# Moving the seven seven-product units of each FFN down-projection pass

## The chip, the cores and the metric

The kernel runs on one core of one Trainium2 chip. The metric is the device time of one execution in microseconds (us), the median of several runs. TensorE is called PE below, VectorE DVE, ScalarE ACT, GpSimd POOL, SyncE SP.

## The reference, cut to what matters

The program is a two-layer decoder trunk on a sequence of 256 positions with a model width of 2048, all in float32: a recurrent block (RG-LRU) and an FFN, then an attention block on shared compressed keys and values and a second FFN. Each FFN is

```
def swiglu(hn, w_in, w_out):
    u = hn @ w_in
    return (jax.nn.silu(u[..., :D_FF]) * u[..., D_FF:]) @ w_out
```

with D_FF = 5632. The change touches only how the last product of this line, `(...) @ w_out` (256x5632 by 5632x2048, the down projection), is cut up, in both FFNs.

## The kernel before, in words

**Precision.** Every float32 operand is split into a high part (`w_hi`, `act_hi`, rounded to fp32r by an ACT copy) and a low part (`raw_lo`, `w_lo`, `act_lo`: the operand minus its high part, by DVE). One block product is three matmuls of 128x128 by 128x512: high by high, high by low, low by high (`product`, L1731).

**Units.** The FFN weights come in loads of 1024 KB, one per unit, through four buffers in turn (`raw[n % 4]`). A unit of the down projection is 256 rows of the weights by 1024 columns, that is 2x2 blocks of weights (two row blocks, two column blocks) by 2x2 blocks of activations (two row blocks of the same index, two token tiles). A plain unit does the 2x2 block product in the usual way: 8 block products, 24 matmuls (`plain_unit`). A sum unit does it with 7 block products, 21 matmuls, of sums of blocks (`sum_unit`; a Strassen-like scheme); its products go into two sets of four PSUM banks, `result` and `shared`.

**What a unit costs the other engines.** For a plain unit ACT makes `w_hi` (L555) and DVE makes `raw_lo` (L1005). For a sum unit of the down projection DVE first makes sums of activation blocks (four small instructions, L1083 to L1089) and of weight blocks (four, L1041 to L1046) in `down_sums` and `sums`; ACT makes the high parts of all of them (L616 to L625); DVE makes the low parts in `down_split` and `split_sums` (L1101, L1051, L1055, L1058). The last of these, L1058, or L1005 for a plain unit, increments `w_lo_done`, for which PE waits before the unit. In every second iteration DVE also makes the low part of four activation tiles (`stationary`, L1031), which PE needs before the next even unit (`st_lo`).

**The passes.** The down projection of an FFN is 44 units, two passes of 22 (`PASS_UNITS`), each pass for 1024 of the 2048 output columns. `DOWN_SUMS` names the units of a pass that are sum units; all others are plain. Units are counted from 0 to 43 below: unit 22 is the first of the second pass.

**Order.** There is no planner. Each engine runs its instructions in the order written; semaphores connect them. In `two_pass`, iteration n of DVE and of ACT prepares unit n + 4: DVE does `stationary` if n is odd, then `down_sums(n + 4)` if that is a sum unit, then `down_split(n + 4)`. ACT does the same with its parts. SP issues the load of unit n when PE has finished unit n - 4 (`chunk_used`); `down_sums` also waits for that, and for the load (`raw_in`). At the end of a pass DVE adds the `shared` banks to `h` (`shared_to_h`, in the iteration of the last sum unit, which stays 17) and the `result` banks (`results_to_h`, L1121, in iteration 21). In the first FFN's second pass ACT also makes squares of `h` (`squares`, L584) in iteration 23.

**The hand-over.** The down projection's first four units are prepared by the last block of the up projection (`up`, `body(FB - 1, False)`, DVE from L1205 on). There DVE does, in order: `shared_add`, the split of unit 1, `down_sums` of unit 2, `result_out` (L1210, L1212, and the gating L1190, after ACT's silu L687), the split of unit 2, the split of unit 3. PE transposes the gated block (`transpose_g`, L1724) in the middle of unit 1.

**Buffers.** Sum tiles of weights alternate between two places (`g_no % 2`), sums of activations between three (`g_no % 3`), where `g_no` counts the sum units.

Of the kernel before, what the change touches and what calls it, by code (L numbers as in the profile page):

```python
# [33 lines left out]
FB = FF // W  # L34
# [47 lines left out]
S_UNITS = (2, 4, 6)  # L82
# [1 line left out]

PASS_UNITS = 2 * FB
DOWN_UNITS = 2 * PASS_UNITS
DOWN_SUMS = (2, 5, 7, 10, 12, 15, 17)

UP_TILES, DOWN_TILES = (0, 1, 2, 3), (0, 2, 1, 3)
SUM_BLOCKS = S_BLOCKS + 2  # L90
SUMS = len(S_UNITS) * S_BLOCKS + 2 * len(DOWN_SUMS)

# [17 lines left out]
def build_program(nc, a, out):  # L110
    x, positions = a["x"], a["positions"]
    ctx = ExitStack()
    with ctx:
# [322 lines left out]
        def stat(c, n=1):  # L436
            return stats[:, c:c + n]
# [66 lines left out]
        def is_sum(i, u):  # L504

            return u in S_UNITS and not (isinstance(i, int) and i in (0, FB))
# [5 lines left out]
        def down_sum(n):  # L512

            return n % PASS_UNITS in DOWN_SUMS

        def down_sum_no(n):

            half, v = divmod(n, PASS_UNITS)
            return len(DOWN_SUMS) * half + DOWN_SUMS.index(v)

        def down_unit_no(f, n):

            return SUMS * f + 3 * S_BLOCKS + down_sum_no(n)
# [20 lines left out]
        def _(act):  # L544
# [55 lines left out]
            def gT_out(i, n, banks):  # L600

                act.wait_ge(gT_mm, n)
                for a, bank in enumerate(banks):
                    e = A.activation(feat[:, bass.ds(4 * i + 2 * a, 2), :],
                                     bank[:, :].rearrange("p (a b) -> p a b", a=2), ACT.Copy)
                e.then_inc(gT_act, 1)

            def split_sums(m, s, q, e, tiles=UP_TILES, g_no=None):
# [4 lines left out]
                if g_no is not None:  # L613
                    act.wait_ge(g_sum, g_no + 1)
                    j = g_no % (2 * len(DOWN_SUMS)) % 3
                    A.activation(s_hi[:, j, :, :], s_raw[:, j, :, :], ACT.Copy).then_inc(g_sum_hi, 1)  # L616
# [10 lines left out]
            def down_split(f, n):  # L627
# [3 lines left out]
                elif down_sum(n):  # L631
                    g_no = down_sum_no(n)
                    split_sums((DOWN_C[2 * f + 1] + n) // 4, n % 4, down_unit_no(f, n), g_no % 2,
                               DOWN_TILES, 2 * len(DOWN_SUMS) * f + g_no)
                else:
                    split((DOWN_C[2 * f + 1] + n) // 4, n % 4)

            def two_pass(f):
# [9 lines left out]
                for n in range(DOWN_UNITS - 4):  # L648
                    half, v = divmod(n, PASS_UNITS)
                    if n == 0:  # L650
                        gT_out(FB - 1, FB * (f + 1), ps[0:2])
                    if v == DOWN_SUMS[-1]:
                        p1_out(n, half)
# [342 lines left out]
        def _(dve):  # L996
# [77 lines left out]
            def down_sums(f, n):  # L1074

                d, g_no = 2 * f + 1, down_sum_no(n)
                v, o, j = n % PASS_UNITS, 2 * len(DOWN_SUMS) * f + g_no, g_no % 3
                m, s = (DOWN_C[d] + n) // 4, n % 4
                dve.wait_ge(gT_act, FB * f + v // 2 + 1)
                dve.wait_ge(chunk_used, 4 * m + s - 3)  # L1080
                a11, a21 = feat[:, 2 * v, 0:P], feat[:, 2 * v, P:SEQ]
                a12, a22 = feat[:, 2 * v + 1, 0:P], feat[:, 2 * v + 1, P:SEQ]
                V.tensor_tensor(s_raw[:, j, 0, :], a22, a21, ALU.subtract).then_inc(g_sum_step, 1)  # L1083
                V.tensor_tensor(s_raw[:, j, 2, :], a11, a21, ALU.subtract)
                dve.wait_ge(g_sum_step, 2 * o + 1)
                V.scalar_tensor_tensor(out=s_raw[:, j, 1, :], in0=s_raw[:, j, 0, :], scalar=-1.0, in1=a11,
                                       op0=ALU.mult, op1=ALU.subtract).then_inc(g_sum_step, 1)
                dve.wait_ge(g_sum_step, 2 * o + 2)
                V.tensor_tensor(s_raw[:, j, 3, :], a12, s_raw[:, j, 1, :], ALU.add).then_inc(g_sum, 1)  # L1089
                sums(m, s, down_unit_no(f, n), g_no % 2, DOWN_TILES)  # L1090
# [97 lines left out]
            def up(f, c0, d):  # L1188
                def gated(t, src):
                    return V.scalar_tensor_tensor(out=gtmp[:, t, :], in0=src, scalar=stat(RS + 2 * (d + 1) + t),  # L1190
                                                  in1=gtmp[:, t, :], op0=ALU.mult, op1=ALU.mult)

                def following(i, u):

                    i, u = i + u // 4, (u + 4) % 8
                    m, s = 2 * i + ((c0 + u) // 4), u % 4
                    if isinstance(i, int) and i == FB:
                        down_split(f, u)
                    elif is_sum(i, u):
                        if u != S_UNITS[0]:  # L1200
                            sums(m, s, unit_no(f, i, u), s // 2)
                        split_sums(m, s, unit_no(f, i, u), s // 2)
                    else:
                        split(m, s, to=raw_lo)

                def result_out(i, result):

                    dve.wait_ge(chunk_used, 8 * i + (c0 + 8))
                    for t in range(NT):
                        V.tensor_tensor(gtmp[:, t, :], gtmp[:, t, :], result[2 * t][:, :], ALU.add).then_inc(c_gate, 1)  # L1210
                    for t in range(NT):
                        k = V.tensor_tensor(mix[:, t, :], result[2 * t + 1][:, :], mix[:, t, :], ALU.subtract)  # L1212
                    k.then_inc(r_done, 1)
                    dve.wait_ge(r_done, i + S_BLOCKS * f)
                    dve.wait_ge(silu_done, i + (FB * f + 1))
                    for t in range(NT):
                        k = gated(t, mix[:, t, :])
                    k.then_inc(g_done, 1)

                def body(i, odd):  # L1220
                    result, shared = banks_of(odd)
                    for u in range(8):
                        if u in (3, 4) and isinstance(i, int) and i == FB - 1:
                            stationary(u - 3, act_slot(u - 3), DOWN_G0[d + 1] + u - 2)
                        if u == 6:
                            shared_add(shared, i + (SUM_BLOCKS * f - 1), i + (FB + 2) * f)
                            following(i, 5)
                            if isinstance(i, int) and i == FB - 1:
                                down_sums(f, S_UNITS[0])
                            else:  # L1230
                                sums(2 * i + (c0 // 4 + 2), 2, unit_no(f, i + 1, 2), 1)
                            continue
                        if u == 7:
                            result_out(i, result)
                            following(i, 6)
                        if u != 5:
                            following(i, u)

                for u in range(8):
                    if u == 1:  # L1240
                        act_tiles(d, 3)
                    if u == 2:

                        dve.wait_ge(side_copied, 3 * f + 3)
                        a11, a21 = side_a[:, :, 0, 0:P], side_a[:, :, 0, P:SEQ]
                        a12, a22 = side_a[:, :, 1, 0:P], side_a[:, :, 1, P:SEQ]
                        V.tensor_tensor(side[:, :, 0, :], a22, a21, ALU.subtract).then_inc(u_side, 1)
                        V.tensor_tensor(side[:, :, 2, :], a11, a21, ALU.subtract).then_inc(u_done, 1)
                        dve.wait_ge(u_side, 2 * f + 1)
                        V.scalar_tensor_tensor(out=side[:, :, 1, :], in0=side[:, :, 0, :], scalar=-1.0, in1=a11,  # L1250
                                               op0=ALU.mult, op1=ALU.subtract).then_inc(u_side, 1)
                        dve.wait_ge(u_side, 2 * f + 2)
                        V.tensor_tensor(side[:, :, 3, :], a12, side[:, :, 1, :], ALU.add).then_inc(side_done, 1)
                    if u == 4:
                        dve.wait_ge(side_hi, f + 1)
                        V.tensor_tensor(s_lo, side, s_hi.bitcast(F32), ALU.subtract).then_inc(side_lo, 1)
                    if u == 6:
                        sums(c0 // 4 + 2, 2, unit_no(f, 1, 2), 1)
                        continue
                    if u == 7:  # L1260

                        dve.wait_ge(chunk_used, c0 + 8)
                        dve.wait_ge(silu_done, FB * f + 1)
                        gated(0, ps[1][:, :])
                        gated(1, ps[3][:, :]).then_inc(g_done, 1)
                        following(0, 6)
                    following(0, u)
                with dve.Fori(0, S_BLOCKS // 2 - 1) as j:
                    body(2 * j + 1, True)
                    body(2 * j + 2, False)  # L1270
                body(FB - 2, True)
                body(FB - 1, False)

# [846 lines left out]
```

## Time and profile before

| | |
|---|---|
| time, median of 3 runs (lowest, highest) | 1996.44 us (1996.17, 1996.79) |
| profiled execution: its own time | 1996.43 us |
| profiled execution: its span | 1994.6 us |
| PE busy, share of the span | 1974.2 us, 99% |
| PE weight load busy | 1683.8 us, 84% |
| DVE busy | 1649.1 us, 83% |
| ACT busy | 1136.6 us, 57% |
| first FFN, down projection (units 0 to 43) | about 786 to 1020 us |
| second FFN, down projection | about 1759 to 1991 us |
| TensorE's granted clock | 1.00 of full speed in every slice |

Busy is the time in which an engine has at least one instruction under way. Matmuls are pipelined, with modelled ends: of two matmuls in a row the second starts 0.23 us after the first though each is shown with 0.39 us, so PE looks busy across pauses shorter than that, and pauses of PE are read from the starts of its matmuls. DVE and ACT instructions that wait for nothing also start a little before the one in front has ended.

### The profile page before, as it was taken

Reading aid. Unit: us, or ns where it says so; the run is one execution under the profiler, and the core shown is the slowest. Engines: PE = TensorE matmul, PEld = TensorE weight load, DVE = VectorE, ACT = ScalarE, POOL = GpSimd, SP = SyncE. Lnnn points to the kernel's source line nnn. Section 1 sums busy time; section 2 is a strip of 40 time slices with the busy share of each in tenths; the row PEclk is TensorE's granted clock in tenths of the full one; section 3 lists DMA queues with packets and bytes.
Section 4 is the critical chain, followed back from the end, with each engine's and each line's share of the span. In section 5 each row is a group of like instructions: output and inputs, shape, how many; then the busy total and the mean of one; then the engine's idle time right before and its main releaser. Section 6 shows DMA issues by size and latency. Waiting matters only on the chain.

```text
span 1994.6 us, 26207 instructions
## 1 busy us (share of the span) xinstructions
PE 1974.2 (99%) x9907; PEld 1683.8 (84%) x9907; DVE 1649.1 (83%) x1849; ACT 1136.6 (57%) x1356; POOL 76.5 (4%) x113
## 2 busy tenths in 40 slices
PE   7999999999999999999999999999999999999999
PEld 7999988888888888888898888888888888888887
DVE  6868655788888889999976886468988898899897
ACT  5478445555555556556676664455555555556564
POOL 1140200000000000000001110000000000000000
PEclk9999999999999999999999999999999999999999
DMA  8564663556556565565565435355656556655554
GB/s 278 170 206 158 206 212 115 199 193 202 197 191 209 191 204 194 195 206 192 209 201 169 127 126 185 111 189 192 205 194 205 194 191 208 193 196 203 200 202 168
DMA packets 159488, 378.21 MB, mean 190 GB/s; under 512 B 6154, under 2 KB 10516, under 8 KB 159028
## 3 DMA queue, kind: packets, MB, share of 16 engines
q1 hardware_dynamic: 158960, 376.02, 56.4%
q0 software_dynamic: 272, 1.13, 0.2%
q8 instruction: 48, 0.79, 0.2%
q14 instruction: 28, 0.23, 0.0%
q10 hardware_dynamic: 180, 0.05, 0.0%
HBM read 375.08 MB, written 2.10 MB: 189 GB/s over the span
## 4 chain that ended last, share of the span: by engine, by line
PE 89%; issue 5%; DVE 2%; ACT 1%; DMA 1%; POOL 1%; POOLq 0%; SPq 0%; DVEq 0%; ACTq 0%
PE bank L1731 75%; PE bank L1912 10%; PE bank L1692 2%; PE bank L1724 1%; PE bank L1715 1%; DVE w_lo L1005 0%; POOL stats L1676 0%; DMA h<-in_x 0%; ACT w_hi L555 0%; DMA raw<-in_ffn_w_in 0%; DMA raw<-in_ffn_w_out 0%; PE bank L1894 0%; ACT gtmp L687 0%; ACT w_hi L618 0%; ACT w_lo L621 0%
## 5 line engine op out<-in xcount | busy, mean ns | idle before, releaser
L1731 PE MATMUL bank<-w_hi,act_hi 128*128 128x512 f32 x1840 | 720.2, 391 | 1.7 <-issue 1.5
L1731 PE MATMUL bank<-w_hi,act_lo 128*128 128x512 f32 x1840 | 716.4, 389 | 0.0
L555 ACT ACTIVATE w_hi<-raw 128x2048 fp32r<-128x2048 f32 (+2 forms) x271 | 509.8, 1884 | 331.6 <-DMA raw<-in_ffn_w_in 149.5
L1731 PE MATMUL bank<-raw_lo,act_hi 128*128 128x512 f32 x1584 | 616.4, 389 | 0.0
L1005 DVE TENSOR_TENSOR raw_lo<-raw,w_hi 128x2048 fp32r<-128x2048 f32 x176 | 401.8, 2288 | 112.6 <-ACT w_hi L555 110.5
L1731 PEld LDWEIGHTS bank<-w_hi,act_hi 128*128 128x128 f32 x1840 | 345.5, 188 | 74.9 <-issue 2.6
L1731 PEld LDWEIGHTS bank<-w_hi,act_lo 128*128 128x128 f32 x1840 | 345.4, 188 | 72.1
L1731 PEld LDWEIGHTS bank<-raw_lo,act_hi 128*128 128x128 f32 x1584 | 297.5, 188 | 60.5
L1005 DVE TENSOR_TENSOR w_lo<-raw,w_hi 128x2048 fp32r<-128x2048 f32 (+2 forms) x95 | 211.8, 2240 | 84.3 <-ACT w_hi L555 84.0
L1055 DVE TENSOR_TENSOR raw_lo<-raw,w_hi 128x2048 fp32r<-128x2048 f32 x88 | 201.0, 2284 | 0.0
L618 ACT ACTIVATE w_hi<-raw 128x1024 fp32r<-128x1024 f32 x88 | 93.0, 1057 | 130.0 <-DMA raw<-in_ffn_w_in 107.9
L1731 PE MATMUL bank<-w_lo,act_hi 128*128 128x512 f32 x432 | 153.9, 389 | 0.0
L1731 PE MATMUL bank<-w_lo 128*128 128x512 f32 x528 | 148.2, 389 | 0.0
L1912 PE MATMUL bank<-act_hi,w_hi 128*128 128x256 f32 x512 | 145.6, 284 | 0.0
L1912 PE MATMUL bank<-act_lo,w_hi 128*128 128x256 f32 x512 | 145.1, 283 | 0.0
L1912 PE MATMUL bank<-act_hi,w_lo 128*128 128x256 f32 x512 | 145.1, 283 | 0.0
L1731 PE MATMUL bank<-w_hi,w_lo 128*128 128x512 f32 x352 | 122.7, 389 | 0.0
L1731 PEld LDWEIGHTS bank<-w_lo 128*128 128x128 f32 x528 | 99.1, 188 | 20.6
L621 ACT ACTIVATE w_lo<-t_raw 128x1024 fp32r<-128x1024 f32 x88 | 92.5, 1051 | 35.7 <-DVE t_raw L1042 35.7
L1051 DVE TENSOR_TENSOR w_lo<-t_raw,w_lo 128x1024 fp32r<-128x1024 f32 x88 | 107.4, 1220 | 0.0
L1912 PEld LDWEIGHTS bank<-act_hi,w_hi 128*128 128x128 f32 x512 | 98.6, 193 | 0.1
L1912 PEld LDWEIGHTS bank<-act_lo,w_hi 128*128 128x128 f32 x512 | 98.6, 192 | 0.0
(230 smaller groups left out, 2440.5 us busy)
## 6 DMA issues: line engine op xcount, KB each, us to landing
raw<-in_ffn_w_in SPq DMA_DIRECT2D x176, 1024.0 KB, 5.3
raw<-in_ffn_w_out SPq DMA_DIRECT2D x88, 1024.0 KB, 4.9
raw<-in_lru_w_in SPq DMA_DIRECT2D x32, 1024.0 KB, 5.4
raw<-in_lru_w_out SPq DMA_DIRECT2D x16, 1024.0 KB, 5.4
raw<-in_w_o SPq DMA_DIRECT2D x16, 1024.0 KB, 5.0
raw<-in_w_ukv SPq DMA_DIRECT2D x8, 1024.0 KB, 5.4
raw<-in_w_uq SPq DMA_DIRECT2D x8, 768.0 KB, 4.5
raw<-in_w_dkv SPq DMA_DIRECT2D x8, 576.0 KB, 4.3
```

The lines of the kernel that those rows point to most:

```text
L555: A.activation(flat_chunk(w_hi, s, size), flat_chunk(raw, s, size), ACT.Copy).then_inc(w_hi_done, 1)
L618: A.activation(w_hi[s][:, first, :], raw[s][:, first, :], ACT.Copy)
L621: A.activation(sum_hi_tiles(e)[:, 0:2, :], sum_tiles(t_raw, e)[:, 0:2, :], ACT.Copy).then_inc(sum_hi, 1)
L1005: V.tensor_tensor(flat_chunk(to, s, size), flat_chunk(raw, s, size), flat_chunk(w_hi, s, size).bitcast(F32), ALU.subtract).then_inc(w_lo_d ...
L1051: V.tensor_tensor(sum_tiles(w_lo_t, e)[:, 0:2, :], sum_tiles(t_raw, e)[:, 0:2, :], sum_hi_tiles(e)[:, 0:2, :].bitcast(F32), ALU.subtract)
L1055: V.tensor_tensor(flat_chunk(raw_lo, s, KC * W), flat_chunk(raw, s, KC * W), flat_chunk(w_hi, s, KC * W).bitcast(F32), ALU.subtract)
L1692: i = T.matmul(outs[t], x_part, wp, start=first and n == 0, stop=last and n == 2)
L1715: i = T.transpose(hT_psum(d, b, q)[:, t * P:(t + 1) * P], h[:, t, k * P:(k + 1) * P], ident[:, :])
L1724: i = T.transpose(banks[q // 2][:, (q % 2) * SEQ + t * P:(q % 2) * SEQ + (t + 1) * P], gtmp[:, t, q * P:(q + 1) * P], ident[:, :])
L1731: i = T.matmul(bank[:, :], x_part, w_part, start=first and n == 0, stop=last and n == 2)
L1912: i = T.matmul(lru_bank(idx, q), w_part, x_part, start=first and kk == kks[0] and n == 0, stop=last and kk == kks[-1] and n == 2)
```

## The change

`DOWN_SUMS` gets other numbers: there are seven sum units in each pass, as before, but at other places. The first sum unit of a down projection is now unit 4, which `two_pass` prepares in its iteration 0; so the last block of the up projection no longer makes the sums of unit 2.

```
-DOWN_SUMS = (2, 5, 7, 10, 12, 15, 17)
+DOWN_SUMS = (4, 6, 8, 11, 13, 15, 17)
...
                         if u == 6:
                             shared_add(shared, i + (SUM_BLOCKS * f - 1), i + (FB + 2) * f)
                             following(i, 5)
-                            if isinstance(i, int) and i == FB - 1:
-                                down_sums(f, S_UNITS[0])
-                            else:
+                            if not (isinstance(i, int) and i == FB - 1):
                                 sums(2 * i + (c0 // 4 + 2), 2, unit_no(f, i + 1, 2), 1)
                             continue
```

In units from 0 to 43: before, the sum units are 2, 5, 7, 10, 12, 15, 17, 24, 27, 29, 32, 34, 37, 39; after, 4, 6, 8, 11, 13, 15, 17, 26, 28, 30, 33, 35, 37, 39. The same holds for both FFNs. The loads and their order are the same.

## Rows read from the trace of the kernel before

**Rows 1.** Page: busy time, share of span and instructions of each engine

```profile
PE 1974.2 (99%) x9907; PEld 1683.8 (84%) x9907; DVE 1649.1 (83%) x1849; ACT 1136.6 (57%) x1356; POOL 76.5 (4%) x113
```

**Rows 2.** Windows: stretch, length; busy time of PE, PEld, DVE, ACT, POOL; clock; DMA

```profile
820.00:850.00 30.00, 30.00 (x134) 24.86 (x133) 29.80 (x34) 19.39 (x21) 0.00 (x0) 1.00 0.62 211
```

**Rows 3.** Chain that ended last, in order of time: start, length, what

```profile
498.38 41.53 PE bank L1731 x183
...
798.25 0.74 issue
...
891.40 1.15 DVE act_lo L1031
892.59 112.67 PE bank L1731 x495
...
1770.95 0.74 issue
```

**Rows 4.** PE's timeline around units 1 and 2: start, length, engine, line, operation

```profile
793.96 0.39 PE L1731 MATMUL bank<-w_hi,act_lo 128*128 128x512 f32 x1
794.40 0.33 PE L1724 MATMUL bank<-ident,gtmp 128*128 128x128 f32 x1
...
797.86 0.39 PE L1731 MATMUL bank<-w_hi,act_lo 128*128 128x512 f32 x1
798.99 0.47 PE L1731 MATMUL bank<-w_hi,act_hi 128*128 128x512 f32 x1 [0.74 <-issue]
```

**Rows 5.** DVE's timeline in the hand-over from the up to the down projection

```profile
786.39 0.29 DVE L1083 TENSOR_TENSOR t_raw<-feat_all 128x128 f32<-128x128 f32 x1
...
789.98 1.27 DVE L1210 TENSOR_TENSOR gtmp<-gtmp,bank 128x512 f32<-128x512 f32 x2
...
792.93 1.42 DVE L1190 SCALAR_TENSOR_TENSOR gtmp<-utmp,stats,gtmp 128x512 f32<-128x512 f32 x2 [0.48 <-ACT gtmp L687]
...
798.20 0.68 DVE L1058 TENSOR_TENSOR w_lo<-t_raw,w_lo 128x512 fp32r<-128x512 f32 x1
```

**Rows 6.** DVE's timeline: one sum unit (5), one plain unit (6), one stationary

```profile
804.34 0.28 DVE L1083 TENSOR_TENSOR t_raw<-feat_all 128x128 f32<-128x128 f32 x1
...
805.27 0.69 DVE L1041 TENSOR_TENSOR t_raw<-raw 128x512 f32<-128x512 f32 x1
...
807.93 0.68 DVE L1101 TENSOR_TENSOR w_lo<-t_raw,w_lo 128x512 fp32r<-128x512 f32 x1
...
811.88 0.69 DVE L1058 TENSOR_TENSOR w_lo<-t_raw,w_lo 128x512 fp32r<-128x512 f32 x1
812.48 2.29 DVE L1005 TENSOR_TENSOR raw_lo<-raw,w_hi 128x2048 fp32r<-128x2048 f32 x1
814.69 1.22 DVE L1031 TENSOR_TENSOR act_lo<-feat_all,act_hi 128x1024 fp32r<-128x1024 f32 x1
815.82 0.28 DVE L1083 TENSOR_TENSOR t_raw<-feat_all 128x128 f32<-128x128 f32 x1
```

**Rows 7.** Timeline at unit 17: DVE's last instruction for it, PE's first matmul

```profile
874.80 0.69 DVE L1058 TENSOR_TENSOR w_lo<-t_raw,w_lo 128x512 fp32r<-128x512 f32 x1
...
876.63 0.39 PE L1731 MATMUL bank<-w_hi,act_hi 128*128 128x512 f32 x1
```

**Rows 8.** Timeline of SP and ACT: loads of units 4 and 20, first reader

```profile
791.66 0.37 SPq L362 DMA_DIRECT2D raw<-in_ffn_w_out  x1
...
876.82 0.37 SPq L362 DMA_DIRECT2D raw<-in_ffn_w_out  x1
...
881.99 1.92 ACT L555 ACTIVATE w_hi<-raw 128x2048 fp32r<-128x2048 f32 x1 [3.85 <-DMA raw<-in_ffn_w_out]
```

**Rows 9.** Timeline at the second pass's start: DVE's result additions, ACT's squares

```profile
911.94 2.47 DVE L1121 TENSOR_TENSOR h<-h,bank 128x512 f32<-128x512 f32 x4
...
917.20 0.61 ACT L584 ACTIVATE utmp<-h 128x512 f32<-128x512 f32 x1
...
919.76 0.19 ACT L584 ACTIVATION_READ_ACCUMULATOR utmp<-h 128x1 f32 x1
```

## The prediction

> **What bounds the kernel now.** I read the busy line first: PE 99%, DVE 83% [rows 1]. By it PE is the bound and DVE has a sixth of its time free. The chain of waits agrees for the long stretches: one block of the up projection is 183 matmuls in 41.53 us [rows 3], 0.227 us from start to start, so a plain unit (24 matmuls) takes PE 5.45 us and a sum unit (21) 4.77 us. But the chain leaves PE at the start of both down projections: "issue" 0.74 us ahead of unit 2 at 798.25 and again at 1770.95 [rows 3]. PE's timeline gives the size: the last matmul of unit 1 starts at 797.86, the first of unit 2 at 798.99, 1.13 where 0.23 is usual: a pause of 0.90 us [rows 4]. DVE's last instruction for unit 2 starts at 798.20 and takes 0.68, so it ends at 798.88, 0.11 before PE goes on [rows 5]. PE waited for DVE. A second, small pause is ahead of the transposes of unit 1 (793.96 to 794.40, 0.21 us too long [rows 4]): they wait for the gating L1190 (792.93, 1.42 us [rows 5]). So I looked at DVE by stretches, and there it is not at 83%: 29.80 us busy of 30 in the middle of the first pass [rows 2]. In the down projection DVE and PE are nearly matched, and what counts is DVE's lead: how long before PE wants a unit its `w_lo_done` has come.
>
> **What a unit costs DVE.** From start to start: a sum unit 804.34 to 812.48, 8.14 us; a plain unit 812.48 to 814.69, 2.21; a stationary 814.69 to 815.82, 1.13 [rows 6]. A stationary stands before each odd unit. This gives the whole account:
> - sum unit to next sum unit two later (one plain, one stationary between): DVE 8.14 + 2.21 + 1.13 = 11.48, PE 4.77 + 5.45 = 10.22. The lead falls by 1.27.
> - sum unit to next sum unit three later, two plain: PE 15.67; DVE 12.56 plus the stationaries. With one (7 to 10, where only unit 9 is odd; 2 to 5, since unit 3's is done before) 13.69, lead up by 1.97; with two (12 to 15, 8 to 11) 14.82, lead up by 0.84.
>
> The account can be tested on the kernel before. After the pause unit 2 has a lead of 0.11. 2 to 5: +1.97; 5 to 7: -1.27; 7 to 10: +1.97; 10 to 12: -1.27; 12 to 15: +0.84; 15 to 17: -1.27. Sum: 1.08 at unit 17. Measured: DVE's last instruction for it ends at 874.80 + 0.69 = 875.49, PE starts it at 876.63: 1.14 [rows 7]. So spacing (3, 2, 3, 2, 3, 2) just fits; the new one is 2, 2, 3, 2, 2, 2.
>
> **The change, part by part (first FFN, first pass).** (1) `down_sums` of the first sum unit leaves the hand-over. It held DVE from 786.39 to 789.98, 3.59 us, ahead of `result_out` [rows 5]. ACT's silu then waits for its split of unit 2 (load issued when up unit 6 is done, near 780.8, landed near 785.7, split 1.92), then takes 1.3, so the gating starts near 788.9 and not at 792.93, and the transposes no longer wait: -0.21. (2) Unit 2 is plain: 2.21 us on DVE and not 8.14, done near 792.6 where PE wants it at 797.89: -0.90. The same count of sum and plain units remains, so PE's own work in a pass is unchanged: 0. (3) What is late next. DVE's split of unit 3 waits for its load (issued one plain unit before the 791.66 of unit 4's [rows 8], at 786.2, plus 5.0 to land, plus ACT 1.92): about 793.2 to 795.4. Four small sums, 0.93 [rows 6], to 796.3; then the weight sums of unit 4 wait for the load issued at 791.66 [rows 8]. A load takes 5.0 to 5.2 us to its first reader (876.82 to 881.99, 5.17 [rows 8]), so 796.7. From there 2.66 for the weight sums and 3.95 + 0.69 for the low parts [rows 6]: `w_lo_done` of unit 4 at 804.0. PE wants it at 797.89 + 2 x 5.45 = 808.8. Lead 4.8. Then 6: -1.27, and -0.3, since DVE reaches the weight sums of 6 at about 808.2 and its load, issued when unit 2 is done (about 803.5), lands at 808.5: 3.2. 8: 2.0. 11: +0.84, less 0.3 for the wait on unit 10's load: 2.5. 13: 1.2. 15: 0.0, a pause of about 0.15 with the 0.11 from semaphore to PE. 17: a full 1.27. Cost of the pass: +1.4 us. (4) Unit 20's wait on a stationary goes: PE would start it at 876.63 + 4.77 + 2 x 5.45 = 892.30 and starts at 892.59, behind the L1031 of 891.40 [rows 3], 0.3 us. That chain starts from the load of unit 20, issued when unit 16 is done, before the new pause at 17, so PE now comes later than it: -0.3. In the second FFN the chain has no such step: 0.
>
> **Second pass.** Before, no pause shows in the chain from 892.59 on (495 matmuls in 112.67 us, 0.228 each) [rows 3]. After, the weight sums of unit 26 wait for its load: unit 22 done, 0.2 after PE starts 23, plus 5.0. DVE gets there at the same time, within 0.1: it has the result additions, 2.47 us [rows 9], and the splits of 24 and 25 in front. So `w_lo_done` of 26 comes 0.2 + 5.0 + 2.66 + 4.64 = 12.5 after PE starts 23, PE wants it after 3 x 5.45 = 16.35: lead 3.8, less than at unit 4 because no transposes lie between. DVE had in the kernel before done the sums of unit 24 in the time that it now spends waiting for loads; that time cannot be saved up, since a load waits for PE four units back. In the second FFN: 28: 2.5; 30: 1.3; 33: 2.1; 35: 0.8; 37: -0.4, a pause of 0.5; 39: 1.27. Together +1.8. In the first FFN ACT has the squares too, 917.20 to 919.95 = 2.75 us [rows 9], in iteration 23, behind the high parts of unit 26: after the load of 26 ACT needs some 5.1 for its high parts and a stationary (an estimate), 2.75, and 1.92 for unit 27's split [rows 8], 9.8 in all, and DVE is there after 2.66 + 4.55 + 1.13 = 8.3. DVE waits 1.4, and all later leads are 1.4 less. Then the stationary ahead of PE's unit 28 and 30 decides (1.13 after their neighbours' splits): 28: 0.1; 30: 1.27; 37: 0.6; 39: 1.27. Together +3.2. The squares' wait isn't in the trace before; bounds 0 (ACT is early) and 2.75 (all of it lands on DVE); I take 1.4, from the order of ACT's work.
>
> **Sum.** New pauses: 1.4 + 3.2 in the first FFN, 1.4 + 1.8 in the second: +7.8. Each pause makes the next start 0.08 late (the trace before shows it at 798.99, an instruction of 0.47 for the usual 0.39 [rows 4]): ten of them, +0.8. Removed: 0.21 + 0.90 + 0.08 twice, 0.3 once: -2.7 (the second FFN has the same pause of unit 2, 0.74 in the chain [rows 3]). Net +5.9; both FFNs end on PE and what follows starts from there, so it all reaches the end. The profiled execution took 1996.43, the median is 1996.44: no correction. 2002.3 us.
>
> The rule that speaks for another result: by the Trainium skill, "Perfetto Trace Analysis", section "Identifying the Most-Contended Engine", occupancy names the engine to work on, the highest first; by it PE (weight loads 84%) is above DVE (83%), and only the pauses removed would count, -2.7. The windows say the shares hide a stretch in which DVE is full [rows 2]. The rule's result is the first rival.
>
> **Rivals.** *A, the lead holds.* If DVE entered the passes with up to 3.2 us more lead than I work out, no later pause would come and only the 2.7 would be seen: 1993.7. It needs loads landing near 2 us after their issue; 5.17 is measured [rows 8]. Chance 0.05. *B, half of it.* Each 0.5 us of lead gained in a pass takes 0.5 off its cost; with about 1 us more everywhere (loads at 4.5, ACT never late) 4 passes give back 4: 1998.2. Speaks for it: nothing shows how DVE runs with loads just in time. Chance 0.13. *C, worse than worked out.* A pause delays the next loads too; where the weight sums then wait on each load, another 0.3 to 0.5 per sum unit in the dense parts is lost, or the squares cost all their 2.75: +3.5, 2005.7. Chance 0.10. *The forecast*, 0.72, with 2000.5 to 2004.
>
> No change can be told within 0.2%, 4 us, so 1992.4 and 2000.4 are the marks. Slower: forecast, C, and a little of B: 0.81. Same: most of A and B: 0.17. Faster would need more than all pauses I found removed: 0.02. The range 1999.0 to 2004.6 leaves out A, part of B and most of C.
>
> **What would show it.** Right: PE goes from unit 1 to unit 2 without a pause; pauses of about 1.3 ahead of units 17 and 39 in both FFNs, and ahead of 30 in the first; the instruction before each ends on DVE L1058 (L1031 for 30); DVE idle about 3 us near 905, waiting on ACT for unit 24, which was not there before; leads at 4 and 26 of 4.8 and 3.8. Wrong: no pause at 17 (A), a lead at unit 4 of 5.8 or more (B), waits of DVE on loads at each sum unit (C).

## The result, and the profile after

The change makes the kernel slower by a quarter of a per cent: 2001.39 us (14 runs, 2000.74 to 2002.03) against 1996.43 us (14 runs, 1995.32 to 1997.84) for the kernel before on the same chip. The ratio is 1.0024, with a 95% interval of 1.0016 to 1.0031. 2002.3 us was forecast. The profiled execution of the changed kernel took 2002.03 us (span 2000.2), so its span is 5.6 us longer than that of before, a little more than the 4.96 between the medians: it is the slowest of the 14, and one late load, told below, accounts for some 1.3 us of it.

The page's busy line, which answers to [rows 1]:

```profile
PE 1974.7 (99%) x9907; PEld 1683.0 (84%) x9907; DVE 1650.6 (83%) x1849; ACT 1136.2 (57%) x1356; POOL 76.5 (4%) x113
```

Instructions are the same in number and every share is the same to the per cent. This line cannot show what happened. The windows of two neighbouring stretches of the first pass can (columns as in [rows 2]):

```profile
820.00:850.00 30.00, 30.00 (x134) 24.84 (x133) 29.72 (x36) 20.32 (x24) 0.00 (x0) 1.00 0.61 210
850.00:880.00 30.00, 29.02 (x127) 23.43 (x126) 29.79 (x34) 18.70 (x20) 0.00 (x0) 1.00 0.62 209
```

DVE is full in both. In the first PE is full too, with the 134 matmuls of [rows 2]; in the second, where DVE finishes unit 13 and prepares the sum units 15 and 17, PE starts 7 fewer, and 7 x 0.227 = 1.6 us. The granted clock is 1.00 in both, so it takes no part. The chain of waits of the same kernel (start, length, what) now runs through DVE there:

```profile
785.96 8.17 PE bank L1729 x36
794.13 0.87 PE bank L1722 x8
795.00 8.19 PE bank L1729 x36
...
862.07 2.29 DVE raw_lo L1055
864.87 2.29 DVE raw_lo L1005
867.16 1.13 DVE act_lo L1031
...
873.55 2.29 DVE raw_lo L1055
...
876.49 21.39 PE bank L1729 x93
```

The first three rows are units 0 to 2: 36 matmuls in 8.17 us, 8 transposes, 36 matmuls in 8.19 us, with nothing between. The "issue" ahead of unit 2 of [rows 3] is gone. Ahead of unit 17 the chain leaves PE and follows DVE back over a sum unit (L1055), a plain unit (L1005) and a stationary (L1031).

PE's timeline at that place and at the same place of the other pass and FFN (start, length, instruction, idle time before it and what ended it); the first row is unit 16's last matmul, the others are the first of units 17, 30, 37 and 39 and of the second FFN's unit 17:

```profile
875.12 0.39 PE L1729 MATMUL bank<-w_hi,act_lo 128*128 128x512 f32 x1
876.49 0.50 PE L1729 MATMUL bank<-w_hi,act_hi 128*128 128x512 f32 x1 [0.98 <-DVE w_lo L1058]
876.82 0.39 PE L1729 MATMUL bank<-raw_lo,act_hi 128*128 128x512 f32 x1
...
946.40 0.50 PE L1729 MATMUL bank<-w_hi,act_hi 128*128 128x512 f32 x1 [0.92 <-DVE act_lo L1031]
983.04 0.50 PE L1729 MATMUL bank<-w_hi,act_hi 128*128 128x512 f32 x1 [0.27 <-DVE w_lo L1058]
994.52 0.50 PE L1729 MATMUL bank<-w_hi,act_hi 128*128 128x512 f32 x1 [0.98 <-DVE w_lo L1058]
...
1851.74 0.50 PE L1729 MATMUL bank<-w_hi,act_hi 128*128 128x512 f32 x1 [0.98 <-DVE w_lo L1058]
```

875.12 to 876.49 is 1.37 us where 0.23 is usual: a pause of 1.14 ahead of unit 17, for which DVE in [rows 7] was ready 1.14 us early. From 983.04 to 994.52, the starts of units 37 and 39, are 11.48 us, DVE's cycle to the hundredth; PE alone would need 10.22. The first matmul after a pause takes 0.50 and the next starts 0.33 behind it (876.82), so that the unit takes 4.90 us in place of 4.77. Each full deficit of 1.27 shows as 1.14 in front of the unit and 0.14 in it.

From the starts of all matmuls, in us: the pauses ahead of units (distance less 0.227), what the transposes wait, what the units behind a pause are longer, and the stretch from the start of unit 0 to that of unit 43:

| | pauses, by unit | sum | transposes | slow starts | unit 0 to 43 |
|---|---|---|---|---|---|
| before, first FFN | 2: 0.90, 20: 0.32, 24: 0.08 | 1.30 | 0.28 | 0.35 | 229.02 |
| before, second FFN | 2: 0.90, 20: 0.05, 42: 0.06 | 1.01 | 0.27 | 0.40 | 226.99 |
| after, first FFN | 15: 0.11, 17: 1.14, 30: 1.08, 37: 0.43, 39: 1.14 | 3.91 | 0 | 0.71 | 231.74 |
| after, second FFN | 15: 0.20, 17: 1.14, 30: 1.13, 37: 0.68, 39: 1.14 | 4.29 | 0 | 0.71 | 230.32 |

Before, all that is lost is 3.61 us, after 9.62: +6.01, and the stretches are 2.72 and 3.33 us longer, +6.05 in all. The spans differ by less, 5.6: the first down projection begins 0.23 earlier, and the stretch between the two is 0.24 shorter.

DVE's timeline of the changed kernel (same columns) shows where its lead comes from and where it is lost:

```profile
786.16 1.28 DVE L1210 TENSOR_TENSOR gtmp<-gtmp,bank 128x512 f32<-128x512 f32 x2
789.12 1.42 DVE L1190 SCALAR_TENSOR_TENSOR gtmp<-utmp,stats,gtmp 128x512 f32<-128x512 f32 x2 [0.48 <-ACT gtmp L687]
...
796.29 0.69 DVE L1041 TENSOR_TENSOR t_raw<-raw 128x512 f32<-128x512 f32 x1 [0.26 <-DMA raw<-in_ffn_w_out]
...
904.70 2.29 DVE L1005 TENSOR_TENSOR raw_lo<-raw,w_hi 128x2048 fp32r<-128x2048 f32 x1 [2.97 <-ACT w_hi L555]
...
923.29 2.29 DVE L1005 TENSOR_TENSOR raw_lo<-raw,w_hi 128x2048 fp32r<-128x2048 f32 x1 [1.23 <-ACT w_hi L555]
...
1887.14 2.29 DVE L1005 TENSOR_TENSOR raw_lo<-raw,w_hi 128x2048 fp32r<-128x2048 f32 x1 [1.07 <-ACT w_hi L555]
```

The gating starts at 789.12 in place of 792.93 [rows 5]; the sums of unit 4 start at 796.29, behind their load. At 904.70 DVE has waited 2.97 us for the split of unit 24, for which it had sums to do before. At 923.29 it waits 1.23 for unit 27, whose split stood behind ACT's squares. At 1887.14, in the second FFN, it waits 1.07 for unit 25, whose load was late (below). The lead (PE's first matmul less the end of DVE's last instruction for it) measured 4.88, 2.95, 1.67, 2.50 and 1.22 at units 4, 6, 8, 11 and 13, and 3.98 and 1.38 at 26 and 28.

### The profile page after: what moved, and what is told of

Read it like the earlier page. It is cut to its first block, busy times and chain, and to the rows that moved or that the text cites. A ratio compares the mean times of both kernels' runs of the same rounds, so it can differ in the third digit from the quotient of the medians.

```text
span 2000.2 us, 26207 instructions
## 1 busy us (share of the span) xinstructions
PE 1974.7 (99%) x9907; PEld 1683.0 (84%) x9907; DVE 1650.6 (83%) x1849; ACT 1136.2 (57%) x1356; POOL 76.5 (4%) x113
## 3 DMA queue, kind: packets, MB, share of 16 engines
q0 software_dynamic: 272, 1.13, 0.2%
## 4 chain that ended last, share of the span: by engine, by line
PE 76%; DVE 13%; issue 7%; DMA 2%; ACT 2%; POOL 1%; POOLq 0%; SPq 0%; DVEq 0%; ACTq 0%
PE bank L1729 61%; PE bank L1910 10%; DVE raw_lo L1055 3%; DVE raw_lo L1005 2%; PE bank L1690 2%; DVE act_lo L1031 1%; DMA raw<-in_ffn_w_out 1%; PE bank L1722 1%; DVE raw L1044 1%; DVE t_raw L1046 1%; DVE t_raw L1041 1%; DVE t_raw L1042 1%; DVE w_lo L1101 1%; DVE w_lo L1058 1%; ACT w_hi L555 1%
## 5 line engine op out<-in xcount | busy, mean ns | idle before, releaser
L1005 DVE TENSOR_TENSOR raw_lo<-raw,w_hi 128x2048 fp32r<-128x2048 f32 x176 | 402.6, 2289 | 114.5 <-ACT w_hi L555 112.4
L1005 DVE TENSOR_TENSOR w_lo<-raw,w_hi 128x2048 fp32r<-128x2048 f32 (+2 forms) x95 | 211.8, 2240 | 86.2 <-ACT w_hi L555 86.1
L1055 DVE TENSOR_TENSOR raw_lo<-raw,w_hi 128x2048 fp32r<-128x2048 f32 x88 | 201.0, 2284 | 0.0
```

Of the source, the lines that this page charges most:

```text
L1005: V.tensor_tensor(flat_chunk(to, s, size), flat_chunk(raw, s, size), flat_chunk(w_hi, s, size).bitcast(F32), ALU.subtract).then_inc(w_lo_d ...
L1055: V.tensor_tensor(flat_chunk(raw_lo, s, KC * W), flat_chunk(raw, s, KC * W), flat_chunk(w_hi, s, KC * W).bitcast(F32), ALU.subtract)
```

## The experiments

The theory is the account of DVE's lead: what a group of units costs is the distance of the sum units, and pauses come where the lead has run out. Its rivals here are A (the new places cost nothing), that the cost comes from the hand-over that was edited, that it comes from loads and not from DVE's work, and that the squares carry it. p1_new, p2_new, half_low and dense ran on one chip beside the kernel before at 1995.77 us (23 runs), the other four on another, beside it at 1996.31 us (29 runs).

### One pass alone: p1_new and p2_new

p1_new takes the new places in the first pass of each FFN only, p2_new in the second only (there with the old hand-over, `down_sums` of unit 2 included).

```
 DOWN_SUMS = (4, 6, 8, 11, 13, 15, 17)
+DOWN_SUMS_2 = (2, 5, 7, 10, 12, 15, 17)
...
-            return n % PASS_UNITS in DOWN_SUMS
+            return n % PASS_UNITS in (DOWN_SUMS_2 if n >= PASS_UNITS else DOWN_SUMS)
```

(In p2_new the two tuples are exchanged.)

> The first pass of each FFN has the new places (4, 6, 8, 11, 13, 15, 17), the second the old ones (24, 27, 29, 32, 34, 37, 39). Theory (DVE's lead): the first passes lose their pauses ahead of unit 2 and of unit 20 (about -2.7 us) and get those ahead of 15 and 17 (1.25 and 1.34 in the changed kernel, with their slow next starts about +3.1): +0.5 us against before, 1996.9. Rival (the lost early preparation of unit 2 is what costs): nearly the whole +5.

> The first pass of each FFN has the old places, the second the new ones. Theory (DVE's lead): the second pass cannot see the hand-over, so all its pauses (ahead of 30, 37, 39) are added and nothing is removed: +5 to +6 us against before, 2001.9. It should be slower than or equal to the changed kernel. Rival (the lost early preparation of unit 2 is what costs): 0.

Measured: p1_new 1995.95 us (11 runs), ratio 1.0002 [0.9993, 1.0011]; p2_new 2001.29 us (7 runs), ratio 1.0029 [1.0017, 1.0040]. The costliest group of matmuls of p1_new, then of p2_new, from the view by lines (count, busy time, mean ns, idle time before them and what ended it):

```profile
L1730 PE MATMUL bank<-w_hi,act_hi 128*128 128x512 f32 x1840 | 720.2, 391 | 2.6 <-DVE w_lo L1059 2.6
```

```profile
L1732 PE MATMUL bank<-w_hi,act_hi 128*128 128x512 f32 x1840 | 722.0, 392 | 5.7 <-DVE w_lo L1059 2.8 <-issue 1.5 <-DVE act_lo L1032 1.4
```

p1_new has pauses at unit 15 (0.42 and 0.52) and 17 (1.15 and 1.13) and elsewhere only one of 0.13, at the second FFN's unit 42: the first pass pays about what its hand-over gives back. p2_new keeps the two pauses of unit 2 (the 1.5 under "issue") and has those of 30, 37 and 39 (0.42 to 1.15). So nearly the whole loss comes from the second passes, which gain nothing, as their entry was already free of pauses; the edited hand-over is not its source.

### Half of the stationary's work away: half_low, half_low_before

half_low is the changed kernel with a cheaper L1031 in the down projections, half_low_before the kernel before with the same edit. Nothing else on DVE, no load and no place of a sum unit differs.

```
-            def stationary(g, slot, n):
+            def stationary(g, slot, n, tiles=4):
...
-                V.tensor_tensor(act_lo[:, slot:slot + 4, :], ...
+                V.tensor_tensor(act_lo[:, slot:slot + tiles, :], ...
...
-                        stationary((n + 3) // 2, act_slot((n + 3) // 2), DOWN_G0[d] + (n + 3) // 2 + 1)
+                        stationary((n + 3) // 2, act_slot((n + 3) // 2), DOWN_G0[d] + (n + 3) // 2 + 1, 2)
```

> The changed kernel, where each stationary of the down projections makes the low part of two activation tiles and not four (the low parts of the other two are left out, so the result differs). It takes about 0.55 us from DVE per two units and leaves loads, ACT, PE and the order alone. Theory (DVE's lead): a sum unit and a plain unit then cost DVE about 10.95 and not 11.48, the lead falls by 0.74 and not 1.27 a pair, no pause is left in either pass: about -2.6 against before, 1993.8, 7 to 8 us less than the changed kernel. Rival (the pauses come from loads that land just in time): unchanged, +5.

> The kernel before, with the same half of the stationaries' low parts left out (the result differs). Control for half_low: what the shorter stationary is worth where the lead never runs out. Theory: only the wait of unit 20 on its stationary goes, about -0.5 us, 1995.3; the pauses ahead of unit 2 stay, since no stationary stands ahead of it. So of the 8 us between the changed kernel and half_low all but 0.5 are the pauses. Rival (a shorter stationary is worth the same in any order): -8.

Measured: half_low 1992.61 us (11 runs), ratio to the kernel before 0.9985 [0.9976, 0.9994]; half_low_before 1995.43 us (11 runs), ratio 0.9995 [0.9986, 1.0004]. First the changed kernel's group of matmuls, then half_low's, and two sum units of half_low's DVE:

```profile
L1729 PE MATMUL bank<-w_hi,act_hi 128*128 128x512 f32 x1840 | 720.6, 392 | 6.7 <-DVE w_lo L1058 4.7 <-DVE act_lo L1031 1.9
```

```profile
L1729 PE MATMUL bank<-w_hi,act_hi 128*128 128x512 f32 x1840 | 720.0, 391 | 0.5 <-DVE act_lo L1031 0.4
```

```profile
863.56 0.69 DVE L1058 TENSOR_TENSOR w_lo<-t_raw,w_lo 128x512 fp32r<-128x512 f32 x1
866.36 0.69 DVE L1031 TENSOR_TENSOR act_lo<-feat_all,act_hi 128x512 fp32r<-128x512 f32 x1
...
874.51 0.68 DVE L1058 TENSOR_TENSOR w_lo<-t_raw,w_lo 128x512 fp32r<-128x512 f32 x1
```

An instruction of 0.69 in place of 1.22 shortens the cycle of two units to 10.95 us (863.56 to 874.51), the deficit from 1.27 to 0.73, and the pauses of units 15, 17, 30 and 37 are gone; one of 0.07 at 39 and one of 0.54 at the second FFN's unit 20 remain (the load of that unit took 5.90 us to land). The loads were not touched and DVE's work was, so the rival that the pauses come from loads is refuted. The same half microsecond taken from the kernel before, at as many places, moves its time by less than can be told. This pair is the clearest of the experiments: the same DVE work is worth some 8 us under the new places (ratios 1.0024 and 0.9985, a difference of 0.0039) and at most 3 under the old. Between the two edited kernels the new places stand 0.0010 lower, about 2 us: the side that the change removes, though the intervals of the two overlap.

### Closer still: dense

```
-DOWN_SUMS = (4, 6, 8, 11, 13, 15, 17)
+DOWN_SUMS = (4, 6, 8, 10, 12, 14, 17)
```

> Seven sum units in each pass at 4, 6, 8, 10, 12, 14, 17: two more pairs two apart and no gap of three before 14. Theory (DVE's lead, the account by pairs): the lead of 4.8 at unit 4 is gone at unit 10; pauses of about 0.6 ahead of 10 and 1.27 ahead of 12 and 14, in the second passes 1.2 to 1.27 ahead of 30 or 32, 34 and 36; in all 11 to 14 of them, +13 to +15 us against before, 2010.5. Rival (only the number of sum units counts, with a fixed price for the new start): +5, as the changed kernel.

Measured: 2009.40 us (5 runs), ratio 1.0068 [1.0055, 1.0082]. Two windows of its first FFN and its group of matmuls:

```profile
850.00:880.00 30.00, 28.03 (x122) 22.53 (x121) 29.80 (x33) 18.08 (x20) 0.00 (x0) 1.00 0.50 175
...
960.00:990.00 30.00, 27.44 (x118) 22.07 (x119) 29.76 (x37) 16.56 (x18) 0.00 (x0) 1.00 0.53 177
```

```profile
L1729 PE MATMUL bank<-w_hi,act_hi 128*128 128x512 f32 x1840 | 721.5, 392 | 11.5 <-DVE act_lo L1031 11.5
```

The rows of before have 134 matmuls in 30 us; here PE starts 122 and 118, while DVE stays full. Each further distance of two costs a pause of 1.05 to 1.15 (units 12, 14, 32, 34 and 36 of both FFNs, 30 of the first); with those of 10 (0.70 and 0.46) and small ones at 20 and 42 they are 14.0 us, and now the stationary comes last before nearly each. 13 to 15 was expected over the kernel before, 13.6 came. Load bandwidth is not the limit here: with more pauses the queues carry less (175 and 177 GB/s against 211 in [rows 2]), and DVE, busy 29.8 us of 30, has next to no time in which it could wait for one.

### The squares: squares_later

The changed kernel with ACT's two squares of the first FFN's second pass moved from iteration 23 to 27, behind that iteration's split.

```
-                    if half == 1 and v == 1 and d < 3:
+                    down_split(f, n + 4)
+                    if half == 1 and v == 5 and d < 3:
                         squares(d, 0)
                         squares(d, 1)
-                    down_split(f, n + 4)
```

> The changed kernel, with ACT's squares of the first FFN's second pass in iteration 27, after the split, and not in 23. Theory: DVE's wait of 1.4 for unit 27's high part goes, so the pause ahead of unit 30 goes; but moved into the dense second half the squares delay other splits: pauses of about 0.3, 1.27, 1.27 ahead of 35, 37, 39 in place of 1.1, 0.4, 1.1. Net -0.3 us against the changed kernel, +4.7 against before. Rival (the squares are what makes the second pass dear): -1.5 to -2.5 against the changed kernel.

Measured: 2001.24 us (7 runs, 1999.76 to 2002.82), ratio 1.0027 [1.0016, 1.0038], against 1.0024 [1.0016, 1.0031] for the changed kernel: no difference that can be told. In the profiled execution (1999.76 us, the fastest of the seven) the pause at unit 30 of the first FFN (1.08) is gone, but the one at 37 is 1.14 in place of 0.43, and the one at 39 stays at 1.14; the small one expected at 35 didn't come (lead 0.06). The pass pays 2.28 us in place of 2.65: a lead kept in one place was spent at the next sum units. The squares set where the lead runs out; they don't set the loss.

Its second FFN, which runs the same instructions as the changed kernel's, has no pause at unit 30 either; that is used below.

### The removed side by itself: early_small, early_small_st

Both start from the kernel before and keep its places. In the last block of the up projection early_small moves the four small activation sums of unit 2, 0.93 us on DVE, ahead of `shared_add`, where DVE waited for ACT anyway. early_small_st also puts the stationary ahead of `shared_to_h` in `two_pass`.

```
                         if u == 6:
+                            if isinstance(i, int) and i == FB - 1:
+                                down_sums(f, S_UNITS[0], big=False)
                             shared_add(shared, i + (SUM_BLOCKS * f - 1), i + (FB + 2) * f)
                             following(i, 5)
                             if isinstance(i, int) and i == FB - 1:
-                                down_sums(f, S_UNITS[0])
+                                down_sums(f, S_UNITS[0], small=False)
...
                     half, v = divmod(n, PASS_UNITS)
+                    if n % 2:
+                        stationary((n + 3) // 2, act_slot((n + 3) // 2), DOWN_G0[d] + (n + 3) // 2 + 1)
                     if v == DOWN_SUMS[-1]:
                         if half and d < 3:
                             dve.wait_ge(h_sq, NB * d + 2)
                         shared_to_h(half)
-                    if n % 2:
-                        stationary((n + 3) // 2, act_slot((n + 3) // 2), DOWN_G0[d] + (n + 3) // 2 + 1)
```

> The kernel before, with the four small activation sums of unit 2 moved ahead of shared_add in the last up block, where DVE idles 1.70 us waiting for ACT. Theory: DVE then reaches the gating and the split of unit 2 0.93 us earlier; both pauses (0.21 ahead of the transposes, 0.90 ahead of unit 2) go in both FFNs: -2.2 us, 1993.6. Rival (PE's pause there has another cause, the evacuation of the transposes by ACT): 0.

> As early_small, and in the iteration of the last sum unit DVE makes the stationary before shared_to_h and not after it. Theory: the wait of unit 20 (0.3 us and a slow start) goes as well: -2.7 us against before, 1993.1, no pause at any unit's start. Rival: shared_to_h, 1.13 us later, makes the next pass's first unit wait, and the gain of the second edit is 0 or negative.

Measured: early_small 1994.15 us (11 runs), ratio 0.9988 [0.9979, 0.9997]; early_small_st 1993.28 us (11 runs), ratio 0.9984 [0.9975, 0.9993]. Both are faster than the kernel before, by 2.2 and 3.0 us; between the two the intervals overlap. DVE's timeline of early_small_st at the hand-over and at unit 20's stationary:

```profile
780.02 0.28 DVE L1084 TENSOR_TENSOR t_raw<-feat_all 128x128 f32<-128x128 f32 x1
781.71 0.69 DVE L1066 TENSOR_TENSOR utmp<-gtmp,bank 128x512 f32<-128x512 f32 x1 [0.67 <-ACT gtmp L709]
...
791.85 1.42 DVE L1195 SCALAR_TENSOR_TENSOR gtmp<-utmp,stats,gtmp 128x512 f32<-128x512 f32 x2
797.12 0.69 DVE L1058 TENSOR_TENSOR w_lo<-t_raw,w_lo 128x512 fp32r<-128x512 f32 x1
...
884.94 1.22 DVE L1031 TENSOR_TENSOR act_lo<-feat_all,act_hi 128x1024 fp32r<-128x1024 f32 x1
886.08 0.68 DVE L1066 TENSOR_TENSOR utmp<-gtmp,bank 128x512 f32<-128x512 f32 x1
```

```profile
L1738 PE MATMUL bank<-w_hi,act_hi 128*128 128x512 f32 x1840 | 719.5, 391 | 0.0
```

And its chain of waits in unit 41 of the first FFN:

```profile
1003.05 0.61 DVE utmp L1071
1003.71 1.09 PE bank L1722 x8
```

The small sums (780.02) go into DVE's wait for ACT, which shrinks to 0.67 us; unit 2's last instruction ends at 797.81 in place of 798.88 [rows 5], though this down projection begins 0.3 us later, the stationary comes before the additions, and the L1738 matmuls have no idle time left. early_small, which moves only DVE's small sums, already has neither pause of the hand-over; so DVE it was for which PE waited there, where the trace before names only "issue" [rows 4], and the rival (ACT's evacuation of the transposes) is refuted. The second edit takes away the pauses ahead of units 20 and 42 (0.11, 0.08 and 0.26 in early_small) and has a price of its own: `shared_to_h` ends later, and the transposes of `h` in unit 41 of the first FFN, which follow its bank reads (L1071), start 0.25 us late, 0.31 with their slow start. From unit 0 to 43 its down projections take 227.41 and 225.32 us, 3.28 less than before. This version beats both kernels, by 3.0 us the one before (1.4 to 5.0 by the interval). It shows that the pauses which the change went after were worth some 3 us and could be had with the lead at units 5 to 17 as before (2.26 at 5, 1.20 at 17).

## Why the prediction came out as it did

**The account of the lead: right.** Its three inputs were a sum unit, a plain unit and a stationary on DVE [rows 6]. The distance from 983.04 to 994.52 less 10.22 is 1.26, the forecast deficit of 1.27 per distance of two. The leads forecast at 4, 6, 8, 11 and 13 were 4.8, 3.2, 2.0, 2.5 and 1.2, and each measured within 0.35 of that. dense and half_low move the deficit's count and its size, and the time follows both.

**The first pass: right.** Pauses of 0.15 and 1.27 were forecast and 0.11 to 0.20 and 1.14 (with 0.14 more inside the unit) came. In the first FFN DVE waited 0.57 us for the load of unit 6 (at 808.42) where 0.3 was forecast. p1_new, with the new places here alone, bears out that the pass about balances: +0.2 us, with an interval that holds 0.

**What is removed: mis-sized.** Forecast -2.7, measured -3.61: unit 2 with its slow start 2.02, unit 20 0.68 (0.3 forecast; it has a share in the second FFN too), the transposes 0.55 (0.42 forecast), and 0.36 at units 24 and 42, which the chain of before does not show and which I had put at nothing (42 is the unit 20 of the second pass). early_small_st confirms the size from the other side: its two down projections are 3.28 us shorter, and the 0.31 that it adds in unit 41 makes that about 3.6.

**The second pass of the first FFN: mechanism right, size a little off.** Forecast +3.2, measured 1.08 + 0.43 + 1.14 = 2.65. The wait on the squares was 1.23, not 1.4, and the lead at 26 was 3.98, not 3.8, so no pause came at 28 and smaller ones at 30 and 37. squares_later shows that even with this wait gone the pass pays at 37.

**The second pass of the second FFN: mis-sized by one late load.** +1.8 was forecast from a load of 5.0 us; 1.13 + 0.68 + 1.14 = 2.95 came. The lead at unit 26 was 2.60, not 3.8. The chain of the changed kernel names the cause:

```profile
1878.61 6.55 DMA raw<-in_ffn_w_out
1885.19 1.93 ACT w_hi L555
```

The load of unit 25 took 6.55 us where [rows 8] show 5.17, and DVE waited 1.07 us for its split (1887.14 above). With 1.2 less lead the pass gets the pause at 30 that was not forecast (1.13); from there on it has the forecast leads again (2.17 at 33, 0.66 at 35), and 37 and 39 pay 1.82 where 1.8 was forecast. The control is squares_later, whose second FFN is unchanged. The same instruction of DVE there starts behind no wait:

```profile
1884.71 2.28 DVE L1005 TENSOR_TENSOR raw_lo<-raw,w_hi 128x2048 fp32r<-128x2048 f32 x1
```

Its load of unit 25 landed after 4.82 us, the leads at 26, 28 and 30 are 3.77, 2.50 and 1.22 (forecast 3.8, 2.5 and 1.3), and its pauses are 0.70 at 37 and 1.10 at 39, 1.80 in all. So the forecast of this pass holds where the load comes in time. The load of unit 25 is late in p2_new too (6.16 us, a lead of 3.00, pauses of 2.59) and, with the old places, in early_small_st (6.51 us, no pause): the new places don't make it late, they make it dear. Why it is late in some of the traces was not tested and stays open.

**The slow next start: mis-sized.** I took 0.08 from the one pause of [rows 4], from its first matmul alone; behind each pause of the changed kernel the whole unit is 0.13 to 0.17 longer: 1.42 for the ten, not 0.8.

**The sum.** Added: forecast 7.8 + 0.8 = 8.6, measured 8.20 + 1.42 = 9.62. Removed: 2.7 and 3.61. Each side was about 1 us too small, and the net, 5.9 and 6.01, agrees in part by that luck. The added side owes some 1.3 us to the late load, which not every execution need have; between the medians the net is 4.96, 0.9 less than was forecast. That the kernel loses about 5 us follows from the mechanism; that the two sums meet within 0.1 does not.

**The rivals.** A needed a lead that never runs out; the pauses at 17 and 39, p2_new and dense refute it. B was a milder form of it: the leads at units 4 and 26 were within 0.2 of the forecast or lower, and nothing like the 1 us more that it needed. C, waits of DVE on loads at each sum unit, shows only in part: 0.26 us at 796.29 for unit 4, 0.57 at 808.42 for unit 6, and the one late load; in the dense part before unit 17 DVE waits for none. By the Trainium skill, "Perfetto Trace Analysis", section "Identifying the Most-Contended Engine", the engine with the highest occupancy is the one to relieve; by that only the removed pauses would have counted, 1993.7 us. The shares stayed at PE 99%, PEld 84% and DVE 83% while the time rose by 5 us, and half_low, which takes from DVE alone, brings it back. Taken over the whole kernel, with PE judged by its weight loads, the rule misled; taken over a window of 30 us (DVE busy 29.80, weight loads 24.86 [rows 2]) it points to DVE.

## What to carry to other kernels

Where two engines take nearly the same time per group of units, the order of the heavy ones is an account: the supplier's lead rises with each wide distance and falls with each narrow one, and a pause comes where it would go below zero. Spread the heavy units as evenly as the account allows, work it out from three durations before trying an order, and look for the supplier's idle stretch in windows, not in the shares of the whole. A pause at the start of a stage is better taken away by moving small work into a wait that exists already than by moving a heavy unit into a dense part; and lead can't be saved up when each load waits for a buffer a few units back.

## What the runs showed that was not expected

- A pause costs the consumer a little in itself, whether it lasts 0.11 or 1.14 us: in the changed kernel the first matmul behind it is shown with 0.50 us, not 0.39, the next starts 0.33 to 0.34 behind it, not 0.23, and the whole unit is 0.13 to 0.17 us longer. Why is not shown.
- The time from issue to landing of a 1024 KB load is not one number: the chain of the changed kernel has 4.83, 4.93, 5.18 and 6.55 us in the down projections. Half of such loads of each kernel land within 5.0 us, nine in ten within 5.3, and one to four of 84 take 5.5 to 6.6. One of these stands at the same place in all ten traces, the load of unit 43 of the second FFN (6.40 to 6.57 us); it brings no pause.
- Leads of the same sum unit in the two FFNs of the changed kernel agree to 0.35 us except behind such a load (3.98 and 2.60 at unit 26), so one late load can move a forecast by this account by about 1 us per pass.
